# A two-block transformer kernel: order of the conv weights, start of the second delta-rule chain, and the beat at which column sums and decay rows stand

## The reference, cut to what matters

```python
z = h @ w_in                                     # 1024 -> qkv 1536, gate 512, a 4, b 4, cfm 1024
qkv = silu(causal_dwconv(qkv, gdn_conv_w))       # 4 taps
q, k = l2norm(q), l2norm(k)                      # 4 heads of 128, x * rsqrt(sum(x*x) + eps)
g = -exp(a_log) * softplus(a + dt_bias); beta = sigmoid(b)
# gated delta rule in 8 chunks of 64 tokens, gc = cumsum(g) within a chunk:
decay = where(causal, exp(gc_i - gc_j), 0)
L = where(strict, (k*beta) @ k.T * decay, 0)
u, w = solve(I + L, [v*beta, k*beta*exp(gc)])    # unit lower triangular, 64 x 64
attn = q @ k.T * decay
for each chunk:                                  # the scan, state S of 128 x 128 per head
    v_new = u - w @ S
    o = (q*exp(gc)) @ S + attn @ v_new
    S = S*exp(g_last) + k_dec.T @ v_new
o = rmsnorm(o) * silu(gate)
c = silu(layernorm(causal_dwconv(glu(cfm_in), 31 taps)))
y = concat(o, c) @ w_out
```

## Time and profile before

| | us |
|---|---|
| median of 3 runs (lowest, highest) | 1790.82 (1787.44, 1794.62) |
| the profiled execution, its span | 1793.55, 1791.6 |
| PE busy, share of the span | 1743.1, 97% |
| DVE busy | 1044.6, 58% |
| ACT busy | 689.9, 39% |
| POOL busy | 197.4, 11% |

### The profile page before, as it was taken

One profiled execution on the slowest core, in us unless ns is written; L12 is line 12 of the kernel. 1 busy time (PEld: TensorE's weight loads), 2 busy tenths in 40 slices (PEclk: granted clock), 3 DMA queues, 4 the chain that ended last, 5 costly groups with the idle time before them and its releaser, 6 DMA issues.

```text
span 1791.6 us, 23508 instructions
## 1 busy us (share of the span) xinstructions
PE 1743.1 (97%) x9629; PEld 1441.8 (80%) x9629; DVE 1044.6 (58%) x1544; ACT 689.9 (39%) x1035; POOL 197.4 (11%) x165
## 2 busy tenths in 40 slices
PE   9999988899999999999999999999999999999997
PEld 6777776789789888888898887878798878787786
DVE  5677787447428954955876553445556444354445
ACT  4543334345335322322352322232255544253352
POOL 0343643112012000000010000000010000000001
PEclk9799999999999999999999999999999999999999
DMA  5111112242122232332322222222222222222221
GB/s 194 48 49 48 36 60 71 82 153 76 43 71 83 95 111 78 113 99 73 123 94 98 73 95 80 97 82 82 73 84 72 71 78 76 82 83 71 83 71 48
DMA packets 45145, 147.70 MB, mean 82 GB/s; under 512 B 4976, under 2 KB 8944, under 8 KB 45040
## 3 DMA queue, kind: packets, MB, share of 16 engines
q1 hardware_dynamic: 45040, 146.21, 25.1%
HBM read 144.09 MB, written 2.10 MB: 82 GB/s over the span
## 4 chain that ended last, share of the span: by engine, by line
PE 85%; DVE 11%; issue 2%; ACT 1%; POOL 0%; DMA 0%; SPq 0%; DVEq 0%; ACTq 0%; POOLq 0%
PE ps L463 25%; PE ps L458 20%; PE ps L459 20%; PE ps L460 20%; DVE sl L1909 2%; DVE acc L2105 2%; DVE y L2281 1%; DVE ca L1964 1%; DVE xl L2298 1%; DVE h L2291 0%; ACT sh L1264 0%; PE ps L1104 0%; DMA raw<-in_wqkv 0%; DVE ss L2071 0%; DVE pad L1955 0%
## 5 line engine op out<-in xcount | busy, mean ns | idle before, releaser
L1264 ACT ACTIVATE sh<-raw 128x1024 fp32r<-128x1024 f32 x260 | 271.3, 1054 | 446.0 <-PE ps L460 320.9
L1909 DVE TENSOR_TENSOR sl<-raw,sh 128x1024 fp32r<-128x1024 f32 x260 | 326.8, 1265 | 138.3 <-ACT sh L1264 138.2
L458 PE MATMUL ps<-xh,sh 128*128 128x512 f32 (+1 forms) x664 | 267.3, 403 | 0.0
L460 PE MATMUL ps<-xl,sh 128*128 128x512 f32 (+1 forms) x664 | 257.1, 387 | 0.0
L459 PE MATMUL ps<-xh,sl 128*128 128x512 f32 (+1 forms) x664 | 257.0, 387 | 0.0
L458 PE MATMUL ps<-sh,xh 128*128 128x512 f32 x384 | 156.0, 406 | 0.0
L460 PE MATMUL ps<-sl,xh 128*128 128x512 f32 x384 | 150.2, 391 | 0.0
L459 PE MATMUL ps<-sh,xl 128*128 128x512 f32 x384 | 149.9, 390 | 0.0
L458 PEld LDWEIGHTS ps<-xh,sh 128*128 128x128 f32 x664 | 126.5, 190 | 26.6 <-issue 2.4
L460 PEld LDWEIGHTS ps<-xl,sh 128*128 128x128 f32 x664 | 126.7, 191 | 25.4
L459 PEld LDWEIGHTS ps<-xh,sl 128*128 128x128 f32 x664 | 126.7, 191 | 24.0 <-issue 1.7
(11 more groups left out here) (384 smaller groups left out, 3316.5 us busy)
## 6 DMA issues: line engine op xcount, KB each, us to landing
raw<-in_wup SPq DMA_DIRECT2D x44, 512.0 KB, 3.5
raw<-in_wdn SPq DMA_DIRECT2D x24, 512.0 KB, 3.4
raw<-in_rqk SPq DMA_DIRECT2D x16, 512.0 KB, 4.0
raw<-in_rv SPq DMA_DIRECT2D x16, 512.0 KB, 3.5
raw<-in_rg SPq DMA_DIRECT2D x16, 512.0 KB, 4.6
raw<-in_rout SPq DMA_DIRECT2D x16, 512.0 KB, 3.4
raw<-in_sv SPq DMA_DIRECT2D x16, 512.0 KB, 3.4
raw<-in_sg SPq DMA_DIRECT2D x16, 512.0 KB, 3.4
```

The lines of the kernel that those rows point to most:

```text
L458: e.matmul(dst, wh, ah, start=start, stop=False, skip_group_check=True)
L460: return e.matmul(dst, wh, al, start=False, stop=stop, skip_group_check=True)
L1264: e.activation(SH[j % NSPL][:], RAW[j % NRAW][:], ACT.Copy).then_inc(*hi(j))
L1909: e.tensor_tensor(SL[j % NSPL][:], RAW[j % NRAW][:], SH[j % NSPL][:].bitcast(F32), ALU.subtract).then_inc(*lo(j))
```

## The change

1. The six tiles of a pair are streamed in the order keys, values, queries instead of queries, keys, values (`qkv_tile`).
2. Chain 1 is added after slab 12 instead of after slab 14, six beats earlier, on all four engines.
3. `decay` runs one beat later, and `grow` has one head a beat (four beats) instead of two heads a beat (two beats); DVE's subtractions and ACT's exponentials follow.
4. In `chain`, the column sums of the keys have one head a beat and `kk` a beat of its own. The column sums of the queries move into levels 1 and 2, one head each, with their squares in other buffers; `qk` and DVE's product with it move into level 3, the queries' scaling into levels 3 and 4. Chain 0's pieces from `kk` on stand two beats later than before, up to its end.
5. ACT squares the queries at levels 0 and 1, and `gdn_out(0)` waits for chain 1's last query column sums, since they share a buffer.

No engine gets more or fewer matmuls or elementwise operations, but for some small ones that are now one per head, and ACT gets two more loads of a function table.

```diff
+def qkv_tile(n):
+    return (4, 8, 0)[n % 6 // 2] + 2 * (n // 6) + n % 2
...
-        o += [("wqkv", j * 4 + 2 * p + h) for j in range(3) for h in range(2)]
+        o += [("wqkv", qkv_tile(6 * p + i)) for i in range(6)]
...
             def decay():
                 yield
+                yield
                 pe.wait_ge(*dcv["g"])
...
                         t.then_inc(*gmm(("grow", p, h)))
                         rel[6 + h] = [(dcv, ("diff", p, h)), (dca, ("ea", p, h))]
-                    yield
-                yield
+                        yield
+                for _ in range(2):
+                    yield
...
             def chain(p):
-                yield
-                b = bank(A_)
+                for _ in range(1 if p else 3):
+                    yield
+                a = bank(A_)
                 for h in range(2):
                     pe.wait_ge(*gac[(p, "sq", 2 + h)])
                     for tb in range(NB):
...
+                    if h:
+                        t.then_inc(*gmm((p, "cs", 1)))
+                        rel[A_] = [(gdv, (p, "msk"))]
+                    yield
...
-                b = bank(A_)
-                for h in range(2):
-                    pe.wait_ge(*gac[(p, "sq", h)])
-                    for tb in range(NB):
-                        t = one(b[:, 8 + 4 * h + tb:9 + 4 * h + tb], hd(R1[p], h)[:, tb * 128:tb * 128 + 128],
-                                ONE[:, 0:1], False, True)
-                t.then_inc(*gmm((p, "cs", 0)))
...
+                    if n_ in (1, 2):
+                        h = n_ - 1
+                        b = bank(B_)
+                        pe.wait_ge(*gac[(p, "sq", h)])
+                        for tb in range(NB):
+                            t = one(b[:, tb:tb + 1], SQ[h][:, tb * 128:tb * 128 + 128], ONE[:, 0:1], tb == 0, True)
+                        t.then_inc(*gmm((p, "cs", 0, h)))
+                        rel[B_] = [(gdv, (p, "msq", h))]
...
-                if n == 10:
+                if n == 8:
                     fg.add(chain(1))
```

More of the change, by code:

```diff
@@ L677, in chain @@
                     yield
-                b = bank(B_)
-                for h, tb, par in CHUNKS:
-                    c = slice(tb * 128 + par * 64, tb * 128 + par * 64 + 64)
-                    o = (h * 4 + tb) * 64
-                    t = one(b[RR[par], o:o + 64], QK[:, 2 + h, c], QK[:, h, c], True, True)
-                t.then_inc(*gmm((p, "qk")))
-                rel[B_] = [(gdv, (p, "at"))]
                 b = bank(A_)
@@ L703, in chain @@
                     rel[A_] = [(gdv, (p, "xx", n_))]
+                    if n_ in (1, 2):
[6 more added lines that the diff above has]
+                        rel[B_] = [(gdv, (p, "msq", h))]
+                    if n_ == 3:
+                        b = bank(B_)
+                        for h, tb, par in CHUNKS:
+                            c = slice(tb * 128 + par * 64, tb * 128 + par * 64 + 64)
+                            o = (h * 4 + tb) * 64
+                            t = one(b[RR[par], o:o + 64], QK[:, 2 + h, c], QK[:, h, c], True, True)
+                        t.then_inc(*gmm((p, "qk")))
+                        rel[B_] = [(gdv, (p, "at"))]
                     yield
@@ L1349, in decay @@
                     for h in range(2):
+                        if p and h == 0:
+                            relu_exp(0)
                         ac.wait_ge(*dcv[("diff", p, h)])
                         e.activation(hd(R4[p], h), PS[6 + h][:], ACT.Exp).then_inc(*dca(("ea", p, h)))
-                    if p:
-                        relu_exp(0)
+                        yield
+                relu_exp(1)
+                for _ in range(2):
                     yield
-                relu_exp(1)
-                yield
             def relu_exp(p):
@@ L1993, in chain @@
                 A_, B_ = (PS[i] for i in KBANK[p])
-                yield
-                yield
+                for _ in range(2 if p else 4):
+                    yield
                 ve.wait_ge(*gmm[(p, "cs", 1)])
@@ L2797, in decay @@
             def decay():
-                for _ in range(4):
+                for _ in range(6):
                     yield
```

70 lines of the change are left out of this document (38 added, 32 removed).

## The result

The changed kernel takes 1800.57 us (median of 13 runs, 1795.56 to 1814.67); the kernel before took 1790.82 (13 runs, 1787.19 to 1794.78). The ratio is 1.006 with a 95% interval of 1.0039 to 1.0081: slower by 10 us, or 0.6%, and clear of noise. The profiled execution of the changed kernel, with a span of 1793.6 us and 1795.56 us in all, happens to be the fastest of the 13. So its trace tells where each step went, but shows only 2 of the 10 us.

A forecast was written before the change was run, and what follows sets the result against it. PE was taken as the bound, with DVE pacing the memory keys. After +5.2 us up to the keys, -0.7 by their end and -6.6 in the gate slabs gave -7.3 from 1790.8: 1783.5 us, range 1774 to 1798.

The forecast's parts named there:

- both clock terms together: Slabs 5 to 19: half-clock cost falls from 9.2 and 4.4 us to 3.1 and 1.3, -9.2 us.
- Step 1: Slabs 5 to 10: waits of 2.1, 2.6 and 3.0 us, idle +4.2 us; half-clock cost 3.1 instead of 9.2.
- Step 2: Slabs 11 to 19: +9.9 us of PE's work, waits 9 us against 8.7, half-clock loss 1.3 of 4.4 left.
- price of 46%: Share of a half-clock stretch counted as lost, since `grow` takes 3.78 us there and 2.05 at full clock.
- Step 3: Memory keys: DVE sets the pace, its list shortens by 3.2 us; slab 28 starts at 291.3, not 292.05, -0.7 us.
- Step 4: Gate slabs: five pieces of chain 1's scan and a 1.17 us wait go, nothing takes their place, -6.6 us.
- ACT's table loads: Two more loads in slabs 8 to 12, where ACT is busy half of the time, costed at nothing.
- (c): Slabs 10 to 19: DVE becomes the bound, waits 26 us instead of 9, 1800.5 us; chance 0.14.
- (b): Slabs 5 to 10: clock stays down or falls again up to about 88 us, costing 7 more, 1790.5; chance 0.17.
- (a): Slabs 5 to 10: the clock does not fall, another 3.1 us are won, 1780.4 us; chance 0.20.

The follow-up runs named there:

- filled_ahead: Changed kernel plus slab-sized matmuls of unread result, each group but one in a free bank ahead of PE's waits: 1796.30 us, ratio 1.0039.
- start_as_before: Changed kernel with chain 1 started after slab 14, as in the kernel before: 1792.57 us, ratio 1.0009 against the kernel before.
- the second profile: The changed kernel, unedited, run again with another execution profiled (span 1798.0 us): 1799.75 us, ratio 1.0058.
- last_key_first: Changed kernel with DVE's copy of the last memory key ahead of that slab's four taps: 1795.01 us, ratio 1.0038.
- copies_ahead: Changed kernel with DVE's two copies for the decay rows one beat sooner, ahead of the convolutions: 1796.89 us, ratio 1.0044.

## Why the prediction was wrong, point by point

The forecast was 1783.5 us, the result 1800.6. Without its clock terms (-9.2) the forecast put the changed kernel 1.9 us above the kernel before; at equal clock it is 5.4 above. With them it gained 9.2 us by the clock; the clock went the other way, by 0.0043, or 5.2 us at the fitted slope. So by that slope, of 17 us some 14 are the clock and 3 are waits. The split is an estimate: at the 0.7 us of filled_ahead the 5.2 would be 3.

- **The step that failed: "both clock terms together" (steps 1 and 2), -9.2 us.** It took the half-clock stretches of the kernel before away where their cause was spread, and left 1.3 us for one `w`. From 49 us to the first key copy the forecast left 10 us at half clock of the 30.7 before; the two profiles of the changed kernel have 27.3 and 30.7. At the forecast's own price of 46% the term was worth -1.6 us and nothing. For slabs 5 to 10 it was half right (clock 0.91; 13 us at half clock instead of 20, where 7 were forecast), but start_as_before, the same program up to there, had 30.7 us. For slabs 11 to 19 it was wrong (0.95 over 135 us are 13.5 us at half clock, where 3 were forecast and the kernel before had 9.7). For the memory keys, the gate and the part behind 314 us there was no such term at all, though 0.91 over 58.5 us stood there in the first profile.
- **What stood in its place in slabs 11 to 19:** the falls of the kernel before at 179 and 186 us came right behind the sixteen column sums, as step 2 has it, and spreading took those away. But in both profiles of the changed kernel the clock falls within 2 us behind waits. PE's timeline, first profile:

```profile
139.02 0.66 PE L736 MATMUL ps<-idn,qk 128*128 128x128 f32 x4 [2.39 <-DVE km L2067]
...
176.51 1.15 PE L468 MATMUL ps<-ch,u_t 64*64 64x64 f32 x32 [2.13 <-DVE u_t L2040]
...
183.23 0.65 PE L468 MATMUL ps<-ss,u_x 128*64 128x128 f32 x4 [1.73 <-DVE ss L2095]
```

  The clock falls at 140.2, 177.7 and 184.6 us, and once more at 150.4 behind `w`. Step 2 summed its waits rightly but gave them no price in clock. A wait is not enough, though: in the second profile five scan steps between 267 and 295 us wait for 1.40 us each, and the clock stays up.
- **Step 1, waits:** expected 2.1, 2.6 and 3.0 us; measured 1.93, 1.10 and 3.15 in the first profile, 1.93, 2.67 and 3.07 in the second. Right; the 1.10 is short since the clock had fallen at 54.9, so that PE came later to `grow`.
- **Step 2, work:** +9.9 us of chain 1's pieces ahead of the keys. PE's idle time from 121 us to the first key copy was 9.7 us (forecast 9, before 8.7). Right. The first key copy came 5.8 us later than forecast; the clock term was off by 7.6 there, and the waits of step 1 were 1.5 us shorter than forecast in this profile.
- **Step 3:** the eight key copies span 48.3 us (256.14 to 304.48) instead of 51.6, 3.2 less as forecast, and 49.2 in the second profile, 2.4 less. Right; that the first agrees to the tenth is luck, since the last copy's delay and half clock are in it.
- **Step 4:** nothing was to take the place of chain 1's pieces. Two things did: the wait for the last key copy behind four slow taps (up to 2.5 us; the forecast let slab 28 start behind the seventh copy and did not look at slab 29 and the eighth), and the clock. last_key_first shows the first, 2.2 us at equal clock.
- **ACT's table loads** were cost at nothing, with the reason that PE's value transposes do not wait for `ea`. POOL runs its list in order, though, with the power that scales the values behind the mask. In copies_ahead DVE waits 4.67 us for that power and PE's second value transpose 2.77 us for DVE. How much of this the loads bring about is not shown.
- **The rival (c)**, slower at 1800.5, came out by its number but not by its mechanism: idle time in slabs 10 to 19 was 9.7 us and not 26. (b) named the clock, only for slabs 5 to 10 and without a loss beyond zero; something like it did happen in the profiled execution of start_as_before, down from 60.4 to 84.3 us. (a) did not happen in either profile of the changed kernel: at 54.9 us the clock fell behind a wait of 1.93 us between dense runs. The Trainium skill ("TensorE: Matmul & The Clock Gate", HAM oscillation — how this bites in real kernels) has idle gaps longer than this as what brings it down; the trace does not agree.
- **The profiled execution** was taken as typical, with a shift to the median. Both kernels vary with the clock, the changed one more widely (1795.6 to 1815.5 us in 20 runs against 1784.9 to 1797.4 in 123); a forecast in which clock stretches make up most of the sum needs a range for them on the slow side too.

Left open: why a start after slab 14 gives a higher clock than one slab sooner or later, and why the clock falls behind one wait and not behind another of the same length. No experiment isolates either; the four starts only show that it is so.

## What to carry to other kernels

Cost a moved piece at equal clock first, then ask at each place where it makes PE wait or run thin work whether the clock can fall there; do not book the end of a long half-clock stretch as a gain from one profile, since its length differs between executions of the same program. When an engine's list is the bound in a stage, look for the last thing that the next stage takes from it, and put that ahead of work nobody waits for. If PE must wait for some microseconds, matmuls of unread result in a free bank ahead of the wait can pay for themselves, but only if nothing in them waits for what they are to cover.

## What the runs showed of the hardware that was not expected

- The mean granted clock goes with most of the difference between executions of one and the same program: 0.988 at 1795.7 us and 0.973 at 1815.5 us in the changed kernel, 0.992 at 1784.9 and 0.985 at 1795.6 in the kernel before.
- The clock fell with PE idle for less than 2 us at a stretch: at 266.5 us after a wait of 1.41 us with a scan step beside it; and at 54.9 us behind a wait of 1.93 us between slab matmuls. Five places came back in both profiles of the changed kernel: 89, 140, 150, 178 and 185 us (1.1 us later in the second).
- The clock falls in the memory keys (at 266, 280 and 294 us of the first profile) did not hold up the key copies, since DVE paces that stage: they came 6.1 to 7.7 us apart, in the kernel before, at full clock, 6.8 to 8.2.
- Where PE is the bound the lower clock is paid in full view: behind 314 us, 3.4 us more at half clock made the same 7210 matmuls 1.5 to 1.7 us longer, at the same idle time.
